# The differential heads' sums of squares: one float32 product becomes two products of split squares

## What is computed

```python
a = p[:, :, 0] - lam * p[:, :, 1]
diff_out = einsum('bhqk,bhkd->bhqd', a, v)
diff_out = rms_norm(diff_out, diff_norm_g[l]) * (1.0 - lam_init)
mixed = concatenate([fox_out, diff_out], axis=-1)
x = x + einsum('bse,ed->bsd', mixed, w_out[l])
```

## Time and profile before

| | |
|---|---|
| median of 3 runs | 1328.76 us (1328.62 to 1330.7) |
| the profiled execution | 1327.55 us, of which 1325.7 us are the span of the trace |
| TensorE busy | 1304.5 us of the span, 6,361 products |
| VectorE, ScalarE, GpSimd busy | 664.5, 649.3, 675.0 us |
| steps 11 to 36 of the differential heads | about 176 to 247 us of the span |

### The profile page before, as it was taken

How to read it: one execution, slowest core, us unless ns; L and a number is a source line. 1 busy time by engine, 2 the same in 40 slices (tenths; PEclk the granted TensorE clock), 3 DMA queues, 4 the chain that set the end, 5 groups by cost and what they waited for, 6 DMA issues and landing times.

```text
span 1325.7 us, 18925 instructions
## 1 busy us (share of the span) xinstructions
PE 1304.5 (98%) x6361; PEld 1092.7 (82%) x6361; DVE 664.5 (50%) x1237; ACT 649.3 (49%) x1033; POOL 675.0 (51%) x884
## 2 busy tenths in 40 slices
PE   9999999999999999999999999999999999999998
PEld 7887878788888888888887888888888888888887
DVE  7576686752222221112698886867455555551112
ACT  4678666754434333333447766363454444442222
POOL 6423343466555554655465444556655555545550
PEclk9999999999999999999999999999999999999999
DMA  6323332134333333333473232322333333333331
GB/s 183 98 72 88 84 102 86 52 92 124 97 95 95 95 95 96 91 103 93 91 147 97 79 97 68 108 90 83 103 95 106 95 95 95 95 93 102 88 99 64
DMA packets 220189, 126.94 MB, mean 96 GB/s; under 512 B 8627, under 2 KB 215872, under 8 KB 220000
## 3 DMA queue, kind: packets, MB, share of 16 engines
q1 hardware_dynamic: 220103, 126.13, 33.9%
q10 hardware_dynamic: 24, 0.01, 0.0%
HBM read 117.30 MB, written 2.47 MB: 90 GB/s over the span
## 4 chain that ended last, share of the span: by engine, by line
PE 89%; DVE 5%; ACT 3%; issue 2%; DMA 0%; DVEq 0%; SPq 0%; POOL 0%; ACTq 0%; POOLq 0%
PE PS L800 27%; PE PS L801 27%; PE PS L802 27%; PE PS L995 1%; DVE PTL L2047 1%; PE PS L980 1%; PE PS L981 1%; ACT WH L1272 1%; PE PS L1010 1%; DVE PS L2201 1%; PE PS L1011 1%; PE PS L877 0%; DVE SQ L2201 0%; ACT PTH L1420 0%; DVE SS L2201 0%
## 5 line engine op out<-in xcount | busy, mean ns | idle before, releaser
L772 POOL TENSOR_TENSOR WL<-RAW,WH 128x256 fp32r<-128x256 f32 x864 | 667.6, 804 | 620.6 <-ACT WH L1272 620.4
L1272 ACT ACTIVATE WH<-RAW 128x1024 fp32r<-128x1024 f32 (+1 forms) x220 | 229.3, 1044 | 432.4 <-PE PS L802 367.1
L800 PE MATMUL PS<-XH,WH 128*128 128x512 f32 x1072 | 419.2, 391 | 0.0
L801 PE MATMUL PS<-XL,WH 128*128 128x512 f32 x1072 | 417.8, 390 | 0.0
L802 PE MATMUL PS<-XH,WL 128*128 128x512 f32 x1072 | 417.7, 390 | 0.0
L802 PEld LDWEIGHTS PS<-XH,WL 128*128 128x128 f32 x1072 | 201.2, 188 | 42.5
L800 PEld LDWEIGHTS PS<-XH,WH 128*128 128x128 f32 x1072 | 201.3, 188 | 40.9 <-issue 0.9
L801 PEld LDWEIGHTS PS<-XL,WH 128*128 128x128 f32 x1072 | 201.3, 188 | 40.3 <-issue 0.7
L800 PE MATMUL PS<-HH,WH 128*128 128x512 f32 (+1 forms) x374 | 141.0, 377 | 0.0
L802 PE MATMUL PS<-HH,WL 128*128 128x512 f32 (+1 forms) x374 | 140.8, 377 | 0.0
L801 PE MATMUL PS<-HL,WH 128*128 128x512 f32 (+1 forms) x374 | 140.8, 377 | 0.0
(11 more groups left out here) (346 smaller groups left out, 1850.4 us busy)
## 6 DMA issues: line engine op xcount, KB each, us to landing
RAW<-in_w_up SPq DMA_DIRECT2D x66, 512.0 KB, 3.9
RAW<-in_w_in SPq DMA_DIRECT2D x60, 512.0 KB, 3.9
RAW<-in_w_down SPq DMA_DIRECT2D x32, 512.0 KB, 4.0
RAW<-in_w_gate SPq DMA_DIRECT2D x22, 512.0 KB, 3.8
RAW<-in_w_out SPq DMA_DIRECT2D x16, 512.0 KB, 3.8
RAW<-in_w_down SPq DMA_DIRECT2D x16, 384.0 KB, 3.4
QB<-QA SPq DMA_DIRECT2D x24, 128.0 KB
KA<-KA SPq DMA_DIRECT2D x24, 128.0 KB
```

The lines of the kernel that those rows point to most:

```text
L772: ins = pool.tensor_tensor(WL[:, s, cs], RAW[:, s % 2, cs], WH[:, s, cs].bitcast(F32), ALU.subtract)
L800: pe.matmul(out, ah, bh, start=start, stop=False)
L801: pe.matmul(out, ah, bl, start=False, stop=False)
L1272: act.activation(WH[:, s, 0:width], RAW[:, s % 2, 0:width], ACT.Copy).then_inc(w_hi, 1)
```

## The change

The squares get the same split as everything else. ScalarE computes the squares from `ODR` straight into a high part `OSH`; VectorE still computes them in float32 into `SQ`, and then subtracts the high part to get the low part `OSL`, which takes the place of `SQ`'s first half. TensorE adds up the product of `OSH` and that of `OSL` with ones in the reduced format (`ONER`, copied once from `ONE` near the start, between VectorE's copies of the input and the low part of the small forget-gate weights, line 1796). The three `diff_hi` calls move from step 34 to step 35.

```diff
+    OSH = at("OSH", BIG + 24576 + 6144, [P, S], F32R)
+    OSL = at("OSL", 106624, [P, S], F32R)
+    ONER = tiny("ONER", [P, P], F32R)
@@ TensorE, odsum(hd)
                 pe.wait_ge(od_sq, hd + 1)
                 g = o0 + hd
-                pe.matmul(PS[:, OB + g % 2, :], ONE[:, :], SQ[:, 0, :], start=True, stop=True).then_inc(od_ps, 1)
+                pe.matmul(PS[:, OB + g % 2, :], ONER[:, :], OSH[:, :], start=True, stop=False)
+                pe.matmul(PS[:, OB + g % 2, :], ONER[:, :], OSL[:, :], start=False, stop=True).then_inc(od_ps, 1)
@@ ScalarE, attention
                 if i - 4 in ready_after and ready_after[i - 4] % 4 == 3:
                     if kind == "diff":
-                        norm_q = [ready_after[i - 4] // 4]
+                        hd = ready_after[i - 4] // 4
+                        act.wait_ge(od_copy, hd + 1)
+                        if hd:
+                            act.wait_ge(od_ps, hd)
+                        act.activation(OSH[:, :], ODR[:, hd, :], ACT.Square).then_inc(od_sqh, 1)
+                        norm_q = [hd]
@@ ScalarE, attention, after the Ln and Exp of step n + 2
                         act.activation(OF[hd], OF[hd], ACT.Exp, scale=-0.5).then_inc(od_r, 1)
+                if kind == "diff" and i == n + 3:
                     for hd in range(3):
                         diff_hi(hd)
@@ VectorE, start
+        step(dve.tensor_copy(ONER[:, :], ONE[:, :]))
@@ VectorE, attention
-                        dve.tensor_tensor(SQ[:, 0, :], ODR[:, hd, :], ODR[:, hd, :], ALU.mult).then_inc(od_sq, 1)
+                        dve.tensor_tensor(SQ[:, 0, :], ODR[:, hd, :], ODR[:, hd, :], ALU.mult).then_inc(od_sqf, 1)
+                        dve.wait_ge(od_sqf, hd + 1)
+                        dve.wait_ge(od_sqh, hd + 1)
+                        dve.tensor_tensor(OSL[:, :], SQ[:, 0, :], OSH[:, :].bitcast(F32), ALU.subtract).then_inc(od_sq, 1)
```

More of the change, by code:

```diff
@@ L371, in program @@
     od_sum = sem("od_sum")
+    od_sqf = sem("od_sqf")
+    od_sqh = sem("od_sqh")
     od_sq = sem("od_sq")
```

## The result

| kernel | median of its runs | ratio to before, 95% interval | profiled execution | its span |
|---|---|---|---|---|
| before | 1328.62 us (5 runs, 1328.22 to 1330.7) | | 1327.55 us | 1325.7 us |
| after | 1334.98 us (5 runs, 1333.27 to 1335.6) | 1.0040 [1.0030, 1.0051] | 1334.39 us | 1332.6 us |

The change makes the kernel slower, by 6.4 us as the medians say and by 5.3 us as the ratio says; the interval of the ratio is 4.0 to 6.8 us. The forecast was 1333.2 us in a range of 1330.8 to 1336.0 us, with 0.82 on slower. The spans of the two profiled executions differ by 6.9 us.

The account below looks back on a forecast made before the run. TensorE, busy for 98% of the span, was taken to bound the kernel. Heads 0 to 2 at +0.40 us and head 3 at +4.01 us gave +4.4 us, 1333.2 us on the median, range 1330.8 to 1336.0.

Parts of the forecast that it names:

- Float32 sum 0.87 us: TensorE's sum of squares in each differential head: the float32 product alone was taken to cost 0.87 us.
- The pair 0.46 us: The two new reduced-format products replacing each float32 sum on TensorE: 0.46 us together, saving 0.41 us a head.
- Heads 0 to 2, +0.40 us: Later squares against shorter sums: -0.22 us at head 0, +0.31 us each at heads 1 and 2.
- Rival D: At all four sums, ones in the new format are no faster: pair 1.74 us, +9.5 us, 1338.3; chance 0.03.
- The copy of ones, 0 us: VectorE's copy near the start: a loss of 0 to 0.3 us possible, taken as 0.
- ScalarE's order at head 3: ScalarE's list was to run Exp, `WH`, then Square at 244.66 to 245.28, making TensorE wait about 3.3 us.
- rival C: Head 3's squares are in time because ScalarE is free earlier: no loss, 1328.8 us; chance 0.08.
- Head 3's size, +4.01 us: Delay at chunk 0 of `out1`: +3.06 us from the late sum, another 0.95 us waiting there.
- Rival A: The wait at head 3 comes without GpSimd's slowing or a further wait: +2.9 us, 1331.7; chance 0.22.
- the second wait: TensorE before chunk 0 of `out1` waits for the first low part from 249.81 to 250.76: 0.95 us.
- the 1.23 us: VectorE's subtraction at head 3, slowed by GpSimd working beside it: 1.23 us, with 0.69 as low bound.
- Rival B: TensorE's pause at head 3 drops its clock: 1.5 to 3 us more, 1334.7 to 1336.2; chance 0.17.

Follow-up runs that it names:

- square_early: Kernel after, with head 3's Square moved between the three Ln and three Exp of step 34 and `diff_hi` back in step 34; 1330.32 us, ratio to before 1.0008.
- filled_pause: Kernel after, with twelve products whose result nobody reads put in TensorE's pause ahead of head 3's sum; 1333.63 us, ratio to before 1.0036.
- head3_new: Kernel before with the change for head 3 alone, heads 0 to 2 as before; 1335.01 us, ratio to before 1.0039.
- square_ahead_of_wh: Kernel after, with head 3's Square behind the Exp of step 34 and ahead of that step's `WH`, `diff_hi` staying in step 35; 1334.77 us, ratio to before 1.0047.
- layout_only: Kernel before with nothing but the matrix `ONER` in memory and its copy; 1329.7 us, ratio to before 1.0002.

## Why the prediction was right, and where its sizes were off

**Float32 sum 0.87 us: right,** 0.87 measured by doubling it. **The pair 0.46 us:** 0.48 without a wait, but 0.56 after one (248.39 to 248.95), since the second product then comes 0.33 us after the first. At head 3, where the float32 sum had no wait ahead of it, the saving is thus 0.31 us, not 0.41.

**Heads 0 to 2, +0.40 us: right,** 0.47 to 0.52. Here the saving is 0.96 - 0.57 = 0.39 us at each head, since the float32 sum was longer at these places too. From VectorE's copy to the first fill product behind the sum it took 3.21, 2.67 and 2.67 us before (head 0: 180.59 to 183.80) and 3.01 us at each head after: -0.20, +0.34 and +0.34 us, where -0.22, +0.31 and +0.31 were forecast. **Rival D** falls.

**The copy of ones, 0 us:** right in the trace of the kernel after, but in four of nine kernels with it TensorE lost 0.3 to 0.8 us there.

**ScalarE's order at head 3: right.** Exp, `WH`, Square, as worked out, and head 3 carries nearly everything. square_early, which changes only that order and the `diff_hi` with it, takes away 3.9 of 4.5 us. It also shows that **rival C**'s free slot, which I said I did not see, exists: between Ln and Exp. C's price of no loss does not hold for it, though, for the Square there pushes Exp.

**Head 3's size, +4.01 us: measured +4.39 up to chunk 0, +4.46 in all of B.** From the last product before the sum to chunk 0 by terms, predicted (counted from 242.90) and measured:

| term | predicted | after | filled_pause |
|---|---|---|---|
| until the sum starts | 3.70 | 3.34 | 3.34 |
| the pair | 0.46 | 0.56 | 0.57 |
| 12 products of `oa` 7 | 2.75 | 4.34 | 2.76 |
| from there to chunk 0 | 0.95 | none | 1.46 |
| sum | 7.86 | 8.24 | 8.13 |

Two terms were mis-sized. The subtraction `OSL` took 0.81 us, not 1.23: it began 0.47 us after GpSimd's first piece, close to that piece's end, and was held up for 0.12 us only. Then I let GpSimd finish in 3.2 us, so that the last of the three `diff_normed` would be fast again (2.9 us for the three). It took 4.14 us, since VectorE slows it as well, and all three were slow: 248.25 to 251.75, 3.5 us. These errors went opposite ways, so that the forecast's size is closer than its terms; that is luck. **Rival A** falls with them: the second wait is there in filled_pause (1.46 us), and in the kernel after and head3_new slower products at half clock fill it.

**A reading of mine behind the 1.23 us was wrong.** Against an exclusive lock I had said that at head 0 a piece of GpSimd's ended at about 181.5 and the square only at 182.55. That is the row of four pieces divided evenly. The row of before's second and third piece says otherwise:

```profile
180.56 1.43 POOL L772 TENSOR_TENSOR WL<-RAW,WH 128x256 fp32r<-128x256 f32 x2
```

The third piece ended at 181.99, and the square 0.56 us later. That is the distance at which VectorE's rows at head 3 end behind a piece (last section). So head 0 speaks for such a lock, not against it.

**Rival B happened and did not count.** The clock fell, and the 12 products of `oa` 7 took 4.34 us, 1.6 us more than 2.75. I priced that at 1.5 to 3 us on top. What I missed is that the second wait of my own forecast lay right behind and would take up as much of it as it was long (0.95 us as forecast, 1.46 as measured); filled_pause shows that 0.1 us was left. After the pause of 2.30 us (by the weight loads, where the kernel after has 3.37) in square_ahead_of_wh the clock stayed at 1.00.

**The total, +4.4 us predicted:** A and B, the only stretches whose code changed in the attention, give +4.98 us. The medians give 6.4, the ratio 5.3 with an interval from 4.0 to 6.8. What lies between is in start and rest of the traces, where transfers decide and, in some executions, the copy of ones. How much of these 0.3 to 1.4 us belongs to the change is open.

## What to carry to other kernels

Price a shorter instruction together with the engine that has to feed it: here 0.4 us per sum was saved, and one added instruction stood behind a weight conversion in an ordered list and cost ten times that. Before moving work to another engine, read that engine's list at the step where it matters, and either find a place for it or delay the consumer; taking three sums one step later won more than the shorter product. And when two losses follow each other on the same engine (a slow clock, then a wait for a third party that the first does not delay), the first is worth only what it has beyond the second.

## What the hardware showed unexpectedly

**VectorE and GpSimd slow each other in turns.** The rows give the pieces of GpSimd's low part in the kernel after (shortest, median and longest in ns), while VectorE ran `OSL` and the three `ODN` beside it:

```profile
L777 POOL TENSOR_TENSOR WL<-RAW,WH x4: 722/1176/1180, 247.1 to 250.0; 128x256 fp32r<-128x256 f32 x4
```

and for the unit of square_early that ran beside less work of that kind:

```profile
L777 POOL TENSOR_TENSOR WL<-RAW,WH x4: 735/739/1132, 250.8 to 253.3; 128x256 fp32r<-128x256 f32 x4
```

Undisturbed, a piece takes 0.73 us, and three `ODN` in a row start 0.61 us apart (square_early). Together each piece takes 1.18, and the `ODN` start 1.14 us apart and last 1.22. Only the first piece, begun ahead of `OSL`, was as fast as alone (it ended at 247.78). The next two:

```profile
247.75 1.18 POOL L777 TENSOR_TENSOR WL<-RAW,WH 128x256 fp32r<-128x256 f32 x1
...
248.89 1.18 POOL L777 TENSOR_TENSOR WL<-RAW,WH 128x256 fp32r<-128x256 f32 x1
```

The pieces end at 247.78, 248.93, 250.07 and 251.20, VectorE's four rows at 248.34, 249.47, 250.62 and 251.75. Each row of VectorE ends 0.54 to 0.56 us behind a piece, and each further piece 0.58 to 0.60 us behind a row of VectorE; the two add up to the pitch of 1.14. By the pitches GpSimd's own four pieces add up to 0.72 + 3 x 1.14 = 4.14 us, as the row of the timeline has it. The Trainium skill, page "SBUF — State Buffer", section "SBUF: two separate sides", says that the shared ports are an exclusive lock held by whoever starts first. In the prediction I set a shared slowing of 1.23 us against it. These rows fit the page better: the piece that started first lost nothing, and afterwards both took turns at one common pitch. `OSL` lost only 0.12 us, though the piece had 0.25 us to go when `OSL`'s row began, since 0.13 us of a row of 0.69 us can pass ahead of the 0.56.

**The clock after a pause.** The pause of 2.67 us at 107 us left the granted clock at 1.00. The one of 2.48 us in layout_only was followed by half clock:

```profile
106.55 0.19 PEld L1011 LDWEIGHTS PS<-PTH,V 128*128 128x128 f32 x1 [2.48 <-DVE PTL L2049]
```

```profile
108.00:109.00 1.00, 1.00 (x5) 0.90 (x4) 0.37 (x3) 0.98 (x4) 0.24 (x1) 0.50 0.00 0
```

So pauses of nearly the same length can end either way. Here and at head 3 the clock fell 1.2 to 1.3 us after TensorE was back at work; in the earlier trace rows it fell within an idle time. The Trainium skill, page "TensorE: Matmul & The Clock Gate", section "What's actually happening", has two levels, 1.2 and 2.4 GHz, and the lower one after idleness; the granted clock shows 1.00 and 0.50, as that page would have it, and a product came every 0.43 us instead of 0.23. Here too the slow stretch ended up costing nothing: TensorE was 1.06 us behind before ahead of it and 2.61 us at its end, but before has an idle time of 1.69 us at 116.36 us that layout_only does not have, and from 130 us on the distance was 1.04 us.

**No table load ahead of Square.** ScalarE's Square stood behind Ln (square_early) and behind Exp (square_ahead_of_wh), in neither case with a table load ahead of it, while Ln to Exp took a load of 1.28 us each time.
